# Attention in a two-block transformer kernel: negated maxima as a row of the queries, rotary sums and six taps by transfers

## The reference

```python
def apply_rope(x, cos, sin):
    x1, x2 = x[..., :half], x[..., half:]
    return jnp.concatenate([x1 * cos - x2 * sin, x2 * cos + x1 * sin], axis=-1)

def attend(q_nope, q_rope, k_nope, k_rope, v):      # 64 plain and 32 rotary columns a head
    s = (jnp.einsum('bqhd,bkhd->bhqk', q_nope, k_nope)
         + jnp.einsum('bqhr,bkr->bhqk', q_rope, k_rope)).astype(jnp.float32) * SOFTMAX_SCALE
    p = jax.nn.softmax(s, axis=-1).astype(v.dtype)
    return jnp.einsum('bhqk,bkhd->bqhd', p, v)

def conformer_conv(u, dw_w, dw_b, ln_g, ln_b):
    a, gte = jnp.split(u, 2, axis=-1)
    v = a * jax.nn.sigmoid(gte)
    v = dwconv(v, dw_w, dw_b)                        # 31 taps, one weight per channel and tap
    return jax.nn.silu(layer_norm(v, ln_g, ln_b))    # norm over the 512 channels
```

## Time and profile before

| | |
|---|---|
| median of 3 runs | 1103.55 us (1100.03 to 1104.28) |
| the profiled execution | 1100.09 us, span 1098.3 us |
| TensorE (PE) busy | 1074.3 us, 98% |
| VectorE (DVE) busy | 774.1 us, 70% |
| ScalarE (ACT) busy | 564.0 us, 51% |
| GpSimd (POOL) busy | 120.1 us, 11% |
| mean granted TensorE clock | 0.996 of full speed |
| attention, first score of head 0 to the last values | 564.06 to 674.5 us of the span |

### The profile page before, as it was taken

One profiled execution on the slowest core, in us unless ns is written; L12 is line 12 of the kernel. 1 busy time (PEld: TensorE's weight loads), 2 busy tenths in 40 slices (PEclk: granted clock), 3 DMA queues, 4 the chain that ended last, 5 costly groups with the idle time before them and its releaser, 6 DMA issues.

```text
span 1098.3 us, 16381 instructions
## 1 busy us (share of the span) xinstructions
PE 1074.3 (98%) x6595; PEld 890.4 (81%) x6595; DVE 774.1 (70%) x1259; ACT 564.0 (51%) x1022; POOL 120.1 (11%) x152
## 2 busy tenths in 40 slices
PE   7989999999999999999999999999999999999997
PEld 5778888888888788888878777888888888888886
DVE  6978889878677747658886788777665656545427
ACT  6576566656333347764367775575444444431211
POOL 0312111112322000100211113000000000000001
PEclk9999999999999999999999999999999999999999
DMA  9743433345255753131342554222222323252202
GB/s 379 295 186 116 154 136 127 123 173 202 102 200 211 287 212 128 39 126 47 81 94 52 128 123 90 77 77 89 104 105 87 112 80 116 77 209 78 84 32 77
DMA packets 26550, 143.23 MB, mean 130 GB/s; under 512 B 3009, under 2 KB 3433, under 8 KB 12650
## 3 DMA queue, kind: packets, MB, share of 16 engines
q1 hardware_dynamic: 19936, 128.46, 32.7%
q0 software_dynamic: 4176, 7.60, 4.0%
q10 hardware_dynamic: 2362, 6.12, 1.6%
HBM read 132.45 MB, written 2.12 MB: 123 GB/s over the span
## 4 chain that ended last, share of the span: by engine, by line
PE 80%; DVE 9%; ACT 6%; issue 2%; DMA 2%; POOL 1%; ACTq 0%; DVEq 0%; SPq 0%; POOLq 0%
PE PB L185 78%; ACT WH L199 2%; PE PB L193 2%; DVE WL L206 2%; DVE CV L214 1%; POOL UPA L206 1%; DVE RAW L1519 1%; DMA XL<-in_x 1%; DVE PX L237 1%; ACT XL L200 1%; DMA CV<-DG 0%; DMA RAW<-in_wstream 0%; ACT PTA L200 0%; DVE XL L214 0%; DVE TMP L206 0%
## 5 line engine op out<-in xcount | busy, mean ns | idle before, releaser
L185 PE MATMUL PB<-HH,WH 128*128 128x512 f32 (+1 forms) x880 | 338.9, 385 | 3.3 <-DVE HL L206 1.8
L185 PE MATMUL PB<-HH,WL 128*128 128x512 f32 (+1 forms) x880 | 333.2, 379 | 0.0
L206 DVE TENSOR_TENSOR WL<-RAW,WH 128x1024 fp32r<-128x1024 f32 (+3 forms) x172 | 196.4, 1148 | 192.6 <-ACT WH L199 192.1
L185 PE MATMUL PB<-HL,WH 128*128 128x512 f32 (+1 forms) x880 | 331.4, 378 | 0.0
L199 ACT ACTIVATE WH<-RAW 128x1024 fp32r<-128x1024 f32 (+3 forms) x172 | 166.7, 976 | 267.9 <-PE PB L185 235.0
L185 PEld LDWEIGHTS PB<-HH,WH 128*128 128x128 f32 x880 | 166.0, 189 | 36.1 <-issue 2.0
L185 PEld LDWEIGHTS PB<-HH,WL 128*128 128x128 f32 x880 | 165.9, 189 | 31.6 <-issue 0.2
L185 PEld LDWEIGHTS PB<-HL,WH 128*128 128x128 f32 x880 | 166.1, 189 | 29.9 <-issue 0.2
L185 PE MATMUL PB<-WL,AH 128*128 128x512 f32 (+1 forms) x198 | 72.4, 366 | 0.0
L185 PE MATMUL PB<-WH,AH 128*128 128x512 f32 (+1 forms) x198 | 72.4, 366 | 0.0
L185 PE MATMUL PB<-WH,AL 128*128 128x512 f32 (+1 forms) x198 | 72.4, 365 | 0.0
(11 more groups left out here) (308 smaller groups left out, 1747.5 us busy)
## 6 DMA issues: line engine op xcount, KB each, us to landing
RAW<-in_wstream SPq DMA_DIRECT2D x101, 1024.0 KB, 5.0
EARLY<-in_wstream SPq DMA_DIRECT2D x7, 1024.0 KB, 13.6
RAW<-in_wstream SPq DMA_DIRECT2D x5, 768.0 KB, 4.4
CV<-DG POOLq DMA_DIRECT2D x15, 256.0 KB, 3.3
TMP<-TMP POOLq DMA_DIRECT2D x14, 256.0 KB, 3.3
RAW<-in_wstream SPq DMA_DIRECT2D x5, 512.0 KB, 3.6
XL<-in_x SPq DMA_DIRECT2D x2, 1024.0 KB, 6.7
HB<-in_x SPq DMA_DIRECT2D x2, 1024.0 KB, 6.1
```

The source lines that it names most:

```text
L185: return self.put(lambda e: e.matmul(o, l, r, start=start, stop=stop, skip_group_check=skip))
L206: return self.put(lambda e: e.tensor_tensor(o, a, b, op))
```

## The change

It has five parts. (1) The negated maxima become row 96 of QH, and row 96 of the keys is one. `query_row` on TensorE multiplies ones by DGR once a head, and ScalarE copies 32 rows of it into QH. Score products go over 128 rows with no fourth product; the first tile of heads 0, 2, 4, 6 and 7 (`late`) goes over 96 rows with the fourth product, and the row is made behind it. Maxima go over 96 rows. (2) The two rotary products of a query are added, by an accumulating transfer for heads 2 to 7, by VectorE for heads 0 and 1. (3) Of tile 0's 31 taps the last six are ScalarE products added by transfers (`more_product`, `add_more`); VectorE's accumulations go tile by tile, with another spread over the loop. (4) The sums over tiles 0, 1 and 2 and their squares are VectorE's (`norm_sums`). (5) The weight stream and TensorE's order ahead of the loop are changed: query 0, keys 0 and query 1 stand ahead of `u2(3)`, which is blocks 88 and 89. QH 0 and 1 lie in buffers that the last of these tiles reads, so their copies wait for its first two products (`("last", h)`).

```diff
-    for j in (1, 2, 3):
-        u2(j)
-    w(query(0), key(0), value(0), query(1))
+    u2(1)
+    u2(2)
+    w(query(0), key(0), query(1), value(0))
+    u2(3)
...
+    def late(h):
+        return h not in (1, 3, 5)
...
-    CONV_AT = {"75a": 2, "75b": 4, "76": 3, "78": 3, "79": 3, "81": 2, "82": 2, "83": 6, "84": 6, "85": 6, "86": 2, "86b": 2}
+    CONV_AT = {"75a": 2, "75b": 4, "76": 3, "78": 3, "79": 3, "81": 2, "82": 2, "83": 6, "84": 3, "85": 5, "85b": 3, "86": 2, "86b": 3}
     def conv_step(h, t):
         if h > 5:
-            return ((0, 1, 2, 2, 1, 2), (2, 1, 2, 2, 1, 2))[h - 6][t]
-        return ((0, 1, 1, 1, 0, 3), (0, 0, 1, 1, 0, 2))[h % 2][t]
+            return ((0, 1, 1, 1, 1, 1), (1, 1, 1, 1, 1, 0))[h - 6][t]
+        return ((0, 1, 2, 1, 1, 3), (0, 0, 1, 1, 1, 1))[h % 2][t]
+    TAPS_IN = [(0, (0, 2, 3, 5)), (1, (0, 2, 4)), (2, (0, 3, 5)), (3, (0, 4)), (4, (0, 3, 5)), (5, (0, 4)), (6, (0, 2, 3, 5)), (7, (0, 1))]
+    STEPS = {0: 25, 2: 31, 3: 31}
...                                             # conv_plan
-                    two = sorted(left)[:2]
-                    j = two[0] if len(two) == 1 or two[0] != last else two[1]
+                    j = min(left)
...                                             # GpSimd, in the order of h and t
+        def add_more(n):
+            g.wait_ge(S_.a_cv, ("more", n))
+            g.wait_ge(S_.v_cv, ("tap", 0, 24))
+            g.put(lambda e: e.dma_start(CV[:, 0, :], XBUF[n % 2], accum_op=ADD)).then_inc(S_.added[2], ("more", n), by=16)
+        def add_turned(h):
+            g.wait_ge(S_.v_ev, ("q", h))
+            g.put(lambda e: e.dma_start(TMPQ[64:96, :], TMPQ[96:128, :], accum_op=ADD)).then_inc(S_.turned, ("qr", h), by=16)
+        for h in range(8):
+            for t in range(6):
+                if t == 3 and h < 6:
+                    add_turned(h + 2)
+                if product_at(h, t):
+                    add_tap(product_at(h, t))
+                if more_at(h, t) is not None:      # t = 1 and 4 of heads 0, 2, 4
+                    add_more(more_at(h, t))
...                                             # ScalarE's loop
                 power_of(h, t)
+                if t == 0 and late(h):
+                    query_row(h)
+                if t == 5 and h < 7 and not late(h + 1):
+                    query_row(h + 1)
+                if t == 5 and h < 6:
+                    query_high(h + 2)              # at t = 4 before
...                                             # VectorE, query(h) for h of 0 and 1
+            v.tt(QS[64:96, :], z[96:128, :], CS[96:128, NCTX:NKEY], MUL)
+            v.tt(TMPQ[0:96, :], z[0:96, :], CS[0:96, NCTX:NKEY], MUL).then_inc(S_.v_ev, ("q", h))
+            v.wait_ge(S_.v_ev, ("q", h))
+            v.tt(TMPQ[64:96, :], TMPQ[64:96, :], QS[64:96, :], ADD).then_inc(S_.v_s, ("qr", h))
...                                             # VectorE ahead of its loop
         query(0)
-        split(90)
-        query_low(0)
-        split(91)
+        split(88)
+        conv("84")
+        split(89)
         key_low(0)
         key_low(1)
+        conv("85")
+        query_low(0)
+        query(1)
+        conv("85b")
+        query_low(1)
         maxima(0, 0)
         maxima(0, 1)
+        glu(3, 88)
+        split(90)
         maxima(0, 2)
-        split(92)
         maxima(0, 3)
-        query(1)
-        split(93)
-        query_low(1)
+        conv("86")
+        maxima(1, 0)
         conv("86b")
...                                             # TensorE
+        def query_row(h):
+            bk = take_aux(("mr", h), 0)
+            pe.mm(bk, ONESR, DGR[:, :], True, True).then_inc(S_.p_sm, ("mr", h))
...
+            direct = t == 0 and late(h)
+            rows = slice(0, 96 if direct else 128)
-            pe.mm3(bk, KH[h % 3][:, js(t)], KL[h % 3][:, js(t)], QH[h % 3], QL[h % 3], True, False)
-            pe.mm(bk, ONESR, DGR[h % 2][:, :], False, True).then_inc(S_.p_sm, ("s", h, t))
+            op = pe.mm3(bk, KH[h % 3][rows, js(t)], KL[h % 3][rows, js(t)], QH[h % 3][rows, :], QL[h % 3][rows, :], True, not direct)
+            if direct:
+                op = pe.mm(bk, ONESR, DGR[:, :], False, True)
+            op.then_inc(S_.p_sm, ("s", h, t))
+            if direct:
+                query_row(h)
...                                             # in keys(p), between its two parts
+                if p and part:
+                    query_row(2 * p - 1)
...
-        query(0)
-        keys(0)
-        value_tiles(0, 0)
-        value_tiles(0, 1)
+        query(0, 2)
+        keys(0, (3, 0))
+        query(1, 1)
+        for nb in (88, 89):
+            tiles(take(("u2", 3, nb % 2), 2 + nb % 2), nb, hh, hl, (), 8, marks={k: ("last", k) for k in (0, 1)} if nb == 89 else None)
         maxima(0, 0)
         maxima(0, 1)
-        value_tiles(0, 2)
+        value_tiles(0, 0, 0)
+        value_tiles(0, 1, 1)
         maxima(0, 2)
         maxima(0, 3)
-        query(1)
+        value_tiles(0, 2, 2)
```

More of the change, by code:

```diff
@@ L352, in __init__ @@
         self.g_acc = sem("g_acc")
[L353 to L354 removed]
+        self.v_cv, self.a_cv = sem("v_cv"), sem("a_cv")
+        self.added = [sem(f"s_added{i}") for i in range(3)]
+        self.turned = sem("s_turned")
         self.every = [z for z in vars_of(self)]
@@ L480, in build_in @@
     OT = sb("OT", [128, S], F32, c2)
-    DGR = [sb(f"DGR{i}", [128, S], F32R, c2) for i in range(2)]
+    DGR = sb("DGR", [128, S], F32R, c2)
+    QS = sb("QS", [128, S], F32, c2)
     TMP = sb("TMP", [128, 1024], F32, c2)
@@ L612, in product_of @@
         return LANES[k] if k < 2 else (DG[:, :], TMP[:, 0:512])[k % 2]
+    STEPS = {0: 25, 2: 31, 3: 31}
+    XBUF = [ROWS5[:, 6 * 512:7 * 512], ROWS5[:, 4096 + 6 * 512:4096 + 7 * 512]]
     def conv_plan():
-        plan, ends, left, last = {}, {ADDED: "end"}, {0: 0}, None
+        plan, left = {}, {0: 0}
         places = [(p, n) for p, n in CONV_AT.items()] + [((h, t), conv_step(h, t)) for h in range(8) for t in range(6)]
@@ L624, in conv_plan, with more_at, summed @@
                 if left:
-                    two = sorted(left)[:2]
-                    j = two[0] if len(two) == 1 or two[0] != last else two[1]
+                    j = min(left)
                     plan[p].append((j, left[j]))
-                    left[j], last = left[j] + 1, j
-                    if left[j] == 31:
+                    left[j] += 1
+                    if left[j] == STEPS[j]:
                         del left[j]
-                        ends[j] = p
-        return plan, ends
-    CONV, CONV_END = conv_plan()
+        return plan
+    CONV = conv_plan()
+    def more_at(h, t):
+        return h + (t == 4) if h in (0, 2, 4) and t in (1, 4) else None
+    def summed(j):
+        return (S_.added[2], ("more", 5)) if j == 0 else (S_.v_cv, ("cv", j))
     def square_at(j):
-        p = CONV_END[j]
-        at = 48 if p == "end" or j == 3 else 2 if isinstance(p, str) else 6 * p[0] + p[1] + 2
-        return at if at < 44 else None
+        return {0: 32, 2: 21}.get(j)
     def tick_of(nb, t):
@@ L800, in pool_prog, with add_tap @@
         g.memset(VGs[:, :, :, 1, :], 1.0).then_inc(S_.g_s, "vone")
-        for k in range(2, 31):
+        def add_tap(k):
             g.wait_ge(S_.a_cv, ("prod", k))
@@ L1298, in query_high, with no_rest @@
         def query_high(h):
-            a.wait_ge(S_.v_ev, ("q", h))
+            a.wait_ge(*rotated(h))
             if h > 2:
                 a.wait_ge(S_.p_sm, ("s", h - 3, 5))
-            a.copy(QH[h % 3], TMPQ[:, :]).then_inc(S_.a_h, ("q", h))
+            elif h < 2:
+                a.wait_ge(S_.p_sm, ("last", h))
+            a.copy(QH[h % 3][0:96, :], TMPQ[0:96, :]).then_inc(S_.a_h, ("q", h))
+        def no_rest(i):
+            a.wait_ge(*((S_.p_sm, ("last", i)) if i < 2 else (S_.p_blk, 89)))
+            a.act(QL[i][96:128, :], CS[96:128, NCTX:NKEY], ACTF.Identity, scale=0.0).then_inc(S_.a_s, ("rest", i))
         def value_tiles(g, q):
@@ L1379, in act_prog @@
                     maxima(h + 1, t - 1)
+                if h == 0 and t in (2, 3, 4):
+                    split(89 + t)
+                if (h, t) == (0, 5):
+                    no_rest(2)
                 if product_at(h, t):
                     tap_product(product_at(h, t))
+                if more_at(h, t) is not None:
+                    more_product(more_at(h, t))
                 if t == 0 and h % 2 and h < 6:
@@ L2043, in dve_prog @@
                     key_low(h + 2)
-                if t in (0, 2, 3) and h < 7:
-                    maxima(h + 1, (0, 0, 1, 2)[t])
                 if t == 3 and h < 6:
                     query(h + 2)
+                if t in ((2, 3) if h == 0 else (0, 2, 3)) and h < 7:
+                    maxima(h + 1, (0, 0, 1, 2)[t])
+                if t == 3 and h % 2 and h < 6:
+                    split(KEY_BLOCK[(h + 1) // 2] + NW)
+                if t == 2 and 0 < h < 7:
+                    query_low(h + 1)
```

(4 more changed lines are left out.)

144 lines of the change are left out of this document (80 added, 64 removed).

## The result

The changed kernel takes 1105.82 us, median of 9 runs (1103.65 to 1107.75), beside 1101.43 for the kernel before on the same chip (1098.21 to 1104.28, 9 runs). The ratio is 1.0039, 95% interval 1.0027 to 1.0051: some 4.3 us slower, where 2.95 less were forecast. It lies inside the range and within the 0.5% called no change, but on the other side.

What follows compares the result with a forecast made beforehand. TensorE, busy 98%, was taken as the bound, with VectorE late at the start. Terms +3.65 up to head 1's first score and -6.6 from there sum to -2.95: 1103.55 becomes 1100.6 us, 8-in-10 range 1094 to 1108.5.

Steps and rivals of the forecast that it cites:

- The products: 35 fewer 512-column products on TensorE at 0.2275 us each: -7.96 us, all on the path while TensorE stays the bound.
- From head 1 on.: From head 1's first score: 32 products fewer, -7.28 us, plus 0.7 at rows of heads 3 and 5: -6.6 us.
- copy and two handovers take about 1.0: Row copy in heads 1, 3, 5, with 0.7 us of key products as cover: some 0.35 us lost each.
- values cover it in the late heads: In late heads TensorE has the last head's second half of values, 1.5 us, during the row's copy; except head 0.
- six taps by transfers: Six accumulations of 0.78 us leave VectorE, six products of 0.71 come to ScalarE; accumulations then wait for one another.
- rival C: VectorE and ScalarE take over in heads 1 to 5 too, 1.0 us per head given back: 1105.6; chance 0.13.
- The start: VectorE's 23.5 us list, third gate to head 0's fourth maximum, makes TensorE wait: head 1's first score +3.65 us.
- Two signs that I named: TensorE gaps of 3 to 5 us before head 0's first score, ending with reductions; VectorE above 90% in head 0.
- a sign of being wrong: The forecast is wrong if heads 2 to 5 don't get shorter, the sign given for rival C.
- Rotary transfers: Heads 2 to 7: landing 3.3 us after issue loses nothing, without slack on ScalarE; late landings decide from 4.5 us.
- Tile sums: Four additions of 0.69 us move from GpSimd to VectorE beside output products: costed at nothing, 2.8 us without that cover.
- Rival E: TensorE pauses at each change of shape to 96-row products: 4 to 13.7 us more, 1104 to 1114; chance 0.04.

Runs made afterwards that it cites:

- e2: Changed kernel with the row alone undone: every score tile ends with the fourth product again, no row product or copy; 1103.61 us, ratio 1.0022.
- e14: Changed kernel with row and six taps undone together: fourth product in every tile, VectorE does 31 taps of tile 0; 1102.72 us, ratio 1.0018.
- e3: Changed kernel leaving out the last six taps of tile 0, ScalarE's six products and their transfers; 1104.44 us, ratio 1.0023.
- e7: Changed kernel with the six taps alone undone: VectorE does all 31 of tile 0, six accumulations more in heads 6 and 7; 1103.48 us.
- e4: Changed kernel with nine VectorE accumulations moved from ahead of head 0's maxima to heads 6 and 7; 1106.93 us, ratio 1.0042.
- e12: Changed kernel with row copies early, VectorE's 31 taps, second tiles of heads 0, 4, 6 direct, four accumulations moved to heads 6 and 7; 1104.98 us.
- e13: Changed kernel with row copies ahead of exponentials, VectorE's 31 taps, four accumulations moved from ahead of head 0's maxima to heads 2 and 4; 1101.08 us.
- e5: Changed kernel with taps, weight and key parts put behind ScalarE's row copies, rows of heads 1, 3, 5 made earlier; 1108.13 us, ratio 1.0062.
- e11: Changed kernel leaving out 28 convolution accumulations, all that VectorE has in heads 1 to 5; 1105.91 us, ratio 1.0046.
- e6: Changed kernel with the rotary transfers alone undone: VectorE adds the two rotary parts for all heads; 1113.69 us, ratio 1.0111.
- e16: On e13: no row in head 0, keys' high part ahead of ScalarE's taps, four accumulations moved to heads 1, 2 and 3; 1096.51 us, ratio 0.9957.

## Why the prediction was wrong

**The products.** 35 fewer, as said, and where little is late they are worth most of their price: heads 3 and 5 got 1.1 us shorter, for six products of 0.2275, 1.37 us.

**The step that failed: "From head 1 on. -32 x 0.2275 = -7.28, +0.7 at the rows of heads 3 and 5: -6.6 us."** Measured from head 1's first score: +0.25 (4.61 less 1.02 and 3.34). Two of its terms were mis-sized. From the common product the whole loss of 4.6 us comes apart as 2.25 for the row beyond all that its products bring (e2), 1.3 for the taps (e14 against e2), and 1.1 that e14 still has over the kernel before, 0.9 of it ahead of head 0's first score.

The first is the row's round trip. I gave it 0.35 us in heads 1, 3, 5 and nothing in heads 2, 4, 6: "copy and two handovers take about 1.0". I priced the copy as if ScalarE stood free when the row was ready. It had up to a tap product, a weight part, a query copy and two exponentials ahead of it (head 6). The five rows from head 2 on, for which I allowed 0.7, were waited for 0.35, 0.52, 0.92, 1.19 and 0.93 us, 3.9 in sum. TensorE's idle time is 6.5 us over all seven rows, and with the waits that hang on it the row took back 10.2 us (e2). The claim that values cover it in the late heads is what the rows of head 6 refute.

The second is "six taps by transfers", costed only by what VectorE gains. I even wrote that ScalarE gets six products of 0.71 in heads 0, 2 and 4, and counted them under rival C as load; what they cost is their place ahead of the rows of heads 1 and 5 and of the values' copies: 1.4 to 2.3 us by the medians of e3 and e7, 1.9 and 1.8 from the common product, and 0.4 to 1.3 without a row (e14 against e2).

**The start: right in its mechanism, its gaps too large.** VectorE's list from the third gate to the fourth maximum, its first and last entry after:

```profile
543.73 0.69 DVE L207 TENSOR_TENSOR VP<-VP,PB 128x512 f32<-128x512 f32 x1 [0.40 <-ACT VP L201]
...
565.28 1.81 DVE L238 TENSOR_REDUCE PX<-PB 128x1 f32<-128x768 f32 x2
```

It takes 23.4 us (forecast 23.5) and ends at 567.09, less 1.39 of later arrival 565.7; forecast 566.0. In head 0 the first and third maxima products stood at 569.44 and 574.99, less 1.39 at 568.05 and 573.60; forecast 568.65 and 574.3. Head 1's first score moved by 4.36 us instead of 3.65: all came some 0.6 sooner than I said, and then its row was waited for 1.49, where 0.35 was allowed. That the list delays head 0's first score is shown by e4, e12 and e13, which bring it 1.7 us forward by shortening the list. The rest is in head 0, and hangs on the row: without it (e2) head 0 takes 14.61 us, nearly as before. Two signs that I named did not come: ahead of head 0's first score TensorE waits 1.2 us for reductions, not 3 to 5, and in head 0 VectorE is busy for 85%, not above 90. And one came that I had named as a sign of being wrong: heads 2 and 4 got longer.

**Rotary transfers: right for this kernel.** Line 832, issue in ns and from issue to landing:

```profile
L832 POOL DMA_DIRECT2D TMPQ<-TMPQ x6: 792/794/1145, 577.6 to 654.1; - x6
...
DMA to landing us min/median/max: 2.8/3.1/4.1
```

I took 3.3, decisive from 4.5 on; no query copy waited. "Without slack" was wrong here: ScalarE, late itself, began the six copies 5.6 to 8.3 us after the issue, 1.5 us or more behind the slowest landing. Where it came sooner, in e5, and two landings were late, the copies waited 2.8 us together. Four of six issues took 0.79 to 0.80 us, two 1.09 and 1.15. By the rule of the Trainium skill ("SBUF — State Buffer", section "SBUF: two separate sides") each could, as I estimated, have lost one VectorE instruction of 0.78; the two longer issues took 0.3 and 0.36 more, the longest of them while the issue before it (592.75, 0.87) still ran, and nothing waited for them, so by the trace the rule has no part in the time.

**Tile sums: right.** Head 7 to the end is 0.36 us shorter, and no wait for the sums stands there. Four products less make 0.91; what is missing is one new wait of 0.53 in head 7 for an exponential (675.25).

**Rival E: wrong.** Two maxima products (512 and 256 columns) of head 0's stretch, after (96 rows, between products of 128):

```profile
571.04 0.39 PE L186 MATMUL PB<-HH,KL 128*128 128x512 f32 x1
571.27 0.52 PE L186 MATMUL PB<-KH,HH 96*128 96x512 f32 x2
571.62 0.40 PE L186 MATMUL PB<-CH,WH 128*128 128x512 f32 x1
```

and before (128 rows throughout):

```profile
570.92 0.39 PE L185 MATMUL PB<-CH,WL 128*128 128x512 f32 x1
571.15 0.51 PE L185 MATMUL PB<-KH,HH 128*128 128x512 f32 x2
571.49 0.40 PE L185 MATMUL PB<-HH,KH 128*128 128x512 f32 x1
```

0.23 us from start to start into the 96 rows and 0.35 out of them, as 0.23 and 0.34 before: the change of rows costs nothing.

**Rival C** had the right number (1105.6) by luck: it stood for 2 us more than a base of 1103.55, and measured are 4.3 more than 1101.43. It had half of the reason. It named the in-order queue of ScalarE, "a diagonal that waits for a reduction holds the exponentials behind it", but took it for a matter of load on two engines. e11 shows that VectorE's accumulations in heads 1 to 5 have no part in it, e6 that two instructions more ahead of each rotation's end, with the reduction behind them, have a very large one.

**What stays open.** The row of e16 brings 2.7 to 3.3 us less than its 31 products make; 0.9 are the two waits shown, and by the table it brings nothing in heads 4 and 6 and costs 0.5 in head 0; the rest was not taken apart. Parts 4 and 5 of the change were not undone by themselves. The edits of e16 were not run one by one; against e13 heads 0, 1 and 5, where they act, are 1.17, 1.07 and 1.31 us shorter, for 1.1, 0.9 and 1.0 forecast.

## What to carry to other kernels

A product dropped from a full TensorE is worth its place in the stream only as far as what replaces it arrives in time. So follow the replacement through the queue of the engine that makes it, and write down, instruction by instruction, what stands in front of it at that moment: 0.6 us of copy became up to 1.5 us of waiting behind tap products and weight parts, while 21.8 us of VectorE work at other places weighed nothing. And put such a hand-over under work that is long enough, or leave the old form where there is none, as head 0 in e16.

## What was not expected of the hardware

Among the profiles of these kernels the product that all is counted from here starts between 486.4 and 492.8 us, with a granted clock of 0.995 to 0.998 over the execution. Part of that is the clock: near 75 us, behind a wait of TensorE of 2.2 to 2.4 us that all profiles have, the granted clock is at half (1.2 GHz) for 3.4 us in ten of the nineteen, for 6.8 in two, and stays at full speed (2.4 GHz) in seven; the common product starts at 489.8, 490.8 and 488.0 in the mean of the three groups. In e4 and e11 such a stretch of 3.4 us lies in head 0 (571.6 on, behind a wait of 1.1 us), and head 0 is as long as without it (17.74 and 17.75 us for 17.73): TensorE was not what bounded that part. A difference of 1 us in the attention can't be read from spans; counted from that product, stretches that kernels share agree within 0.1 us (head 3: 11.69 to 11.71 in after, e3, e4, e7).
